# Output weights split by contraction rows, and one buffer for the normed rows, in a decoder layer on one core

## The reference, cut to what matters

```python
mix = _hybrid_mixer(h, positions, w_in[l], w_out[l])
h_res = (h_res + gate1 * _rms_norm(mix, g_post_mix[l])).astype(x.dtype)
h2 = _rms_norm(h_res, g_pre_ffn[l]) * (1.0 + scale2) + shift2
ffn = _hier_moe(h2, w_group[l], b_group[l], w_expert[l], b_expert[l],
                w_gate_exp[l], w_up_exp[l], w_down_exp[l])
h_res = (h_res + gate2 * _rms_norm(ffn, g_post_ffn[l])).astype(x.dtype)

# in _hybrid_mixer
mixed = jnp.concatenate([att.astype(h.dtype), ret], axis=-1)
return jnp.einsum('bse,ed->bsd', mixed, w_out)
```

## Time and profile before

| | |
|---|---|
| runs, median of 3 | 684.8 us (684.11 to 686.64) |
| span of the profiled execution | 686.0 us |
| PE busy | 633.2 us (92%), 2400 matmul records |
| DVE busy | 375.3 us (55%) |
| ACT busy | 206.1 us (30%) |
| moved by DMA | 174.70 MB, mean 255 GB/s |

### The profile page before, as it was taken

One profiled execution on the slowest core, in us unless ns is written; L12 is line 12 of the kernel. 1 busy time (PEld: TensorE's weight loads), 2 busy tenths in 40 slices (PEclk: granted clock), 3 DMA queues, 4 the chain that ended last, 5 costly groups with the idle time before them and its releaser, 6 DMA issues.

```text
span 686.0 us, 7088 instructions
## 1 busy us (share of the span) xinstructions
PE 633.2 (92%) x2400; PEld 298.5 (44%) x2400; DVE 375.3 (55%) x721; ACT 206.1 (30%) x411; POOL 100.3 (15%) x96
## 2 busy tenths in 40 slices
PE   1599999999999999999989999989999999988883
PEld 1364444444344444546644556433434453433331
DVE  5765667999786773246863336862323333232055
ACT  1453443334254544431121322111212121221023
POOL 1004333300122221000000000112121211110101
PEclk9999999999999999999989997999999999998998
DMA  9992715240606144070396129799999999999997
GB/s 329 394 374 96 277 28 216 59 187 7 240 0 204 43 147 162 13 241 31 125 383 289 61 86 402 269 370 409 419 421 419 420 419 420 419 418 413 409 411 157
DMA packets 52757, 174.70 MB, mean 255 GB/s; under 512 B 9712, under 2 KB 9712, under 8 KB 41840
## 3 DMA queue, kind: packets, MB, share of 16 engines
q1 hardware_dynamic: 45136, 160.26, 60.3%
q0 software_dynamic: 6160, 12.10, 5.5%
q10 hardware_dynamic: 1424, 1.87, 0.8%
HBM read 168.43 MB, written 15.21 MB: 268 GB/s over the span
## 4 chain that ended last, share of the span: by engine, by line
PE 73%; DVE 11%; DMA 7%; issue 4%; SPq 2%; ACT 1%; POOLq 0%; DVEq 0%; ACTq 0%
PE psum L772 16%; PE psum L1052 15%; PE psum L1113 8%; PE psum L775 8%; PE psum L920 7%; DMA both_bufs<-pair_rows 3%; DMA ring<-in_w_ada 2%; DVE score L1536 2%; PE psum L1025 2%; DVE sm L1535 2%; DVE score L1766 2%; SPq L647 2%; DVE rows L1459 2%; PE psum L877 2%; PE psum L897 1%
## 5 line engine op out<-in xcount | busy, mean ns | idle before, releaser
L772 PE MATMUL psum<-hT,ring 128*128 128x512 f32 (+1 forms) x320 | 135.8, 579 | 0.0
L1052 PE MATMUL psum<-ring,hT 128*64 128x512 f32 (+2 forms) x320 | 92.2, 594 | 1.8 <-DMA ring<-in_w_up_exp 1.4
L772 PEld LDWEIGHTS psum<-hT,ring 128*128 128x128 f32 x320 | 60.2, 192 | 69.4 <-issue 60.1
L775 PE MATMUL psum<-ring,hT 128*128 128x512 f32 x192 | 85.2, 597 | 0.0
L1885 DVE TENSOR_SCALAR work<-work 128x256 f32<-128x256 f32 x16 | 4.6, 290 | 101.8 <-PE psum L1062 76.0
L1248 ACT ACTIVATE both_bufs<-psum 32x512 f32<-32x512 f32 (+2 forms) x68 | 38.3, 563 | 67.7 <-PE psum L772 66.7
L1459 DVE SCALAR_TENSOR_TENSOR rows<-ring,sm,rows 128x512 f32<-128x512 f32 x64 | 55.5, 866 | 1.7
L775 PEld LDWEIGHTS psum<-ring,hT 128*128 128x128 f32 x192 | 35.6, 190 | 44.6 <-issue 44.2
L1052 PEld LDWEIGHTS psum<-ring,hT 128*64 128x64 f32 (+2 forms) x320 | 31.7, 142 | 48.8 <-issue 46.3
L1347 ACT ACTIVATE work<-psum 128x256 f32<-128x256 f32 x17 | 6.5, 383 | 146.7 <-PE psum L1052 146.7
L1113 PE MATMUL psum<-ring,work 128*64 128x512 f32 (+1 forms) x160 | 40.1, 598 | 0.7 <-ACT work L1353 0.7
(11 more groups left out here) (322 smaller groups left out, 912.9 us busy)
## 6 DMA issues: line engine op xcount, KB each, us to landing
ring<-in_w_down_exp SPq DMA_DIRECT2D x20, 1024.0 KB, 18.4
ring<-in_w_in SPq DMA_DIRECT2D x8, 2048.0 KB, 9.3
ring<-in_w_ada SPq DMA_DIRECT2D x8, 2048.0 KB, 13.8
ring<-in_w_gate_exp SPq DMA_DIRECT2D x14, 1024.0 KB, 20.2
ring<-in_w_up_exp SPq DMA_DIRECT2D x14, 1024.0 KB, 23.0
ring<-in_w_ada SPq DMA_DIRECT2D x7, 1024.0 KB, 13.3
ring<-in_w_gate_exp SPq DMA_DIRECT2D x12, 512.0 KB, 15.2
ring<-in_w_up_exp SPq DMA_DIRECT2D x12, 512.0 KB, 15.4
```

Source lines behind the costliest of these rows:

```text
L772: mm = pe.matmul(o[:, at], w[:, k, b * P:(b + 1) * P], hT3[:, k, at], start=(k == 0), stop=(k == KD - 1))
L775: mm = pe.matmul(o[:, :], hT3[:, k, b * P:(b + 1) * P], w[:, k, :], start=(k == 0), stop=(k == KD - 1))
L1052: mm = pe.matmul(o[rows, :], XT[u % 2][:, k, rows], both(GU_SLOT[place])[:, k, :, :], start=(k == 0), stop=(k == KD - 1))
```

## The change

The output weights are loaded by halves of the contraction: slot 1 holds the 512 attention rows (all 1024 columns), slot 2 the 512 retention rows. `wout(b, half)` does one half of the contraction for both banks. PE's order is new: the attention halves of blocks 0, 1 and 2 run ahead, around `turn_ret`; slot 1 is free after block 3's attention half (`wout_half`) and slot 2 after the last block. The banks of the four blocks become 4, 6, 0, 4 (they were 6, 0, 6, 0), and those of `MOD 5` and of the router follow. There is one buffer of normed rows (`H2`, in `work`), so DVE waits before each block for the store of the block before; the squares go to the buffers of `MIXN`. The tail of slot 1 is therefore free earlier, and expert 1's down weights are loaded with those of experts 0 and 3.

```diff
         for b in range(NB):
-            use(("wout", b), (6, 0)[b % 2], 2)
-        use(("MOD", 5, 0), 6)
-        use(("MOD", 5, 1), 7)
+            use(("wout", b), (4, 6, 0, 4)[b], 2)
+        use(("MOD", 5, 0), 0)
+        use(("MOD", 5, 1), 1)
...
-            use(("router", b), 4 + b % 2)
+            use(("router", b), 6 + b % 2)
...
+        def out_rows(what):
+            s = AT[("out", what)] % RING
+            return ring[:, s * SLOT:s * SLOT + KD // 2 * D].rearrange("p (k n) -> p k n", k=KD // 2)
...
-        H2 = [work[:, 2 * D:3 * D], tail(1)[:, 0:D]]
+        H2 = work[:, 2 * D:3 * D]
...
-        JUNK = tail(1)[:, D:2 * D]
...
-                    sp.dma_start(chunk(n), w_out[:, :, what * 512:(what + 1) * 512]).then_inc(landed[s], 16)
+                    half = slice(what * KD // 2, (what + 1) * KD // 2)
+                    sp.dma_start(out_rows(what), w_out[:, half, :]).then_inc(landed[s], 16)
...
-            for e in (0, 3):
+            for e in (0, 1, 3):
                 load_down(sp, e, e, down_in[e])
...
             for b in range(NB - 1):
+                if b == NB - 2:
+                    sp.wait_ge(*used_up(("out", 0)))
+                    load_gate_up(sp, 1, 1, gu_in[1])
                 sp.wait_ge(res_ready, b + 1)
                 sp.dma_start(out_blocks[b], x3[:, b, :]).then_inc(x2_out, 16)
-            for e in (1, 2):
-                sp.wait_ge(*used_up(LAST_IN[e]))
-                load_gate_up(sp, e, e, gu_in[e])
+            sp.wait_ge(*used_up(("out", 1)))
+            load_gate_up(sp, 2, 2, gu_in[2])
...
-            sp.wait_ge(h2_out[1], 16 * (NB // 2))
-            sp.wait_ge(res_sq, NB)
-            load_down(sp, 1, 1, down_in[1])
...
+                    w = out_rows(half)
                     for n in range(2):
                         o = ps[plan.bank[("wout", b)] + n]
-                        w = chunk(AT[("out", n)])
-                        for k in ks:
-                            mixed = (mixA[:, k, :] if k < 4 else hT3[:, k, :])[:, b * P:(b + 1) * P]
-                            mm = pe.matmul(o[:, :], mixed, w[:, k, :], start=(k == 0), stop=(k == KD - 1))
-                    if ks[-1] == KD - 1:
+                        for k in range(KD // 2):
+                            mixed = (mixA if half == 0 else hT3[:, KD // 2:, :])[:, k, b * P:(b + 1) * P]
+                            mm = pe.matmul(o[:, :], mixed, w[:, k, n * 512:(n + 1) * 512],
+                                           start=(half == 0 and k == 0), stop=(half == 1 and k == KD // 2 - 1))
+                    if half == 1:
                         mm.then_inc(wout_done, 1)
+                    elif b == NB - 1:
+                        mm.then_inc(wout_half, 1)
...
-                wout(0, range(KD // 2))
+                wout(0, 0)
+                wout(1, 0)
                 for b in range(NB):
                     turn_ret(b)
+                wout(2, 0)
                 pe.wait_ge(*brought(("rett", NB - 1)))
...
+                wout(0, 1)
+                wout(1, 1)
+                wout(3, 0)
+                turn_x2(0)
+                wout(2, 1)
+                route(0)
+                turn_x2(1)
+                wout(3, 1)
+                route(1)
+                turn_x2(2)
+                route(2)
                 turn_x2(NB - 1)
                 route(NB - 1)
                 mod(5)
-                pe.wait_ge(mix_n, NB)
-                stream(ps[0], 2)
+                pe.wait_ge(lg_ready, NB - 1)
+                stream(ps[6], 2)
...
-                        if b >= 2:
-                            dve.wait_ge(h2_out[b % 2], 16)
+                        if b >= 1:
+                            dve.wait_ge(h2_out[(b - 1) % 2], 16 * ((b - 1) // 2 + 1))
```

More of the change, by code:

```diff
@@ L495, in used_up @@
                 return unit_done, plan.unit[("unit", what, last_block(what))] + 1
-            return wout_done, NB
+            return (wout_half, 1) if what == 0 else (wout_done, NB)
         def rotated(kind):
@@ L907, in project, with wout @@
             def project():
-                def wout(b, ks):
-                    if b == 0 and ks[0] == 0:
-                        pe.wait_ge(att_ready, NB)
-                        land(pe, AT[("out", 0)])
-                        land(pe, AT[("out", 1)])
-                    if ks[0] == 0:
+                def wout(b, half):
+                    if b == 0:
+                        if half == 0:
+                            pe.wait_ge(att_ready, NB)
+                        land(pe, AT[("out", half)])
+                    if half == 0:
                         take(pe, ("wout", b))
+                    w = out_rows(half)
                     for n in range(2):
                         o = ps[plan.bank[("wout", b)] + n]
-                        w = chunk(AT[("out", n)])
-                        for k in ks:
-                            mixed = (mixA[:, k, :] if k < 4 else hT3[:, k, :])[:, b * P:(b + 1) * P]
-                            mm = pe.matmul(o[:, :], mixed, w[:, k, :], start=(k == 0), stop=(k == KD - 1))
-                    if ks[-1] == KD - 1:
+                        for k in range(KD // 2):
[3 more added lines that the diff above has]
+                    if half == 1:
                         mm.then_inc(wout_done, 1)
+                    elif b == NB - 1:
+                        mm.then_inc(wout_half, 1)
                 def turn_x2(b):
@@ L985, in project @@
                 mm.then_inc(early_done, 1)
-                stream(ps[0], 5)
+                stream(ps[6], 5)
             def late_rows():
@@ L1313, in _ @@
                             act.wait_ge(wout_done, b + 1)
-                            a.activation(JUNK, psum[:, w:w + D], ACT.Square, accum_out=ssm[:, b:b + 1]).then_inc(squared, 1)
+                            a.activation(MIXN[b % 2], psum[:, w:w + D], ACT.Square, accum_out=ssm[:, b:b + 1]).then_inc(squared, 1)
                             act.wait_ge(squared, 2 * b + 1)
@@ L1324, in _ @@
                             act.wait_ge(res_ready, b + 1)
-                            a.activation(JUNK, x3[:, b, :], ACT.Square, accum_out=ss2[:, b:b + 1]).then_inc(squared, 1)
+                            a.activation(MIXN[(b + 1) % 2], x3[:, b, :], ACT.Square, accum_out=ss2[:, b:b + 1]).then_inc(squared, 1)
                             act.wait_ge(squared, 2 * b + 2)
@@ L1873, in _ @@
                         link(v.reciprocal(ss2[:, b:b + 1], r2[:, b:b + 1]))
[L1874 to L1876 removed]
+                        if b >= 1:
+                            dve.wait_ge(h2_out[(b - 1) % 2], 16 * ((b - 1) // 2 + 1))
+                        link(v.scalar_tensor_tensor(out=H2, in0=x3[:, b, :], scalar=ss2[:, b:b + 1],
                                                     in1=S2, op0=ALU.mult, op1=ALU.mult))
[L1878 removed]
+                        v.tensor_tensor(H2, H2, T2, ALU.add).then_inc(h2_ready, 1)
                     routing()
```

16 lines of the change are left out of this document (2 added, 14 removed).

## The result

| | median us | runs | least to most |
|---|---|---|---|
| before | 685.07 | 4 | 684.11 to 686.64 |
| after | 678.33 | 4 | 677.93 to 680.17 |

The ratio is 0.9909, with an interval of 0.989 to 0.9928. The forecast was 677.8 us, 7.0 less than before; measured were 6.7 less (685.07 less 678.33). The profiled execution of the changed kernel has a span of 676.9 us against 686.0.

A forecast was written before the change was run, and what follows sets the result against it. Expert stage bound by weight transfers and nearly as much by PE, its start set by the chain before routing. Projection terms 0.85 + 2.31 + 1.15 + 0.69 + 1.99 = 6.99, others 0, gave 677.8 us; range 673.5 to 681.3.

The forecast's parts named there:

- Start, 0.85: Projection's start: block 0 uses banks already free and starts as the retention matmuls end, 0.85 us less.
- Wait for the retention rows, 2.31, and for the copies, 0.69: Projection: attention halves of blocks 1 and 2 fill PE's waits around the retention transposes, 2.31 and 0.69 us less.
- Transposes, 1.15: Retention transposes in the projection: 2.2 us instead of 3.37, once not paced by DVE and a slow clock; 1.15 less.
- Clock drop, 1.99: Projection matmuls behind the transposes: the 1.2 GHz stretch goes with the idle time before it, 1.99 us less, bounds 0 and -1.99.
- The router stretch, 0, with up to 3.4 more as a rival: Between projection's end (T) and routing: same stretch, 1.2 GHz drop left in place, 0; without it up to 3.4 us less.
- The buffer of normed rows, 0: DVE's wait for a store before reusing the single buffer: no wait, 0; bounds 0 and +2.6 us.
- The transfers, 0: Expert 1's weight loads issued earlier, off the chain: 0 by themselves; bounds 0 and -0.5 us.
- After the routing, everything moves by the whole: Expert stage: weight stream and PE's units both move by the whole 7.0 us; the last wait of 3.44 stays.
- (a): Rival: full clock through the router stretch, 10.4 us less in all, 674.4 us; chance 0.18.
- (b): Rival: part given back before routing, by a 2.6 us buffer wait or remaining slow clock and transposes (3.1); 680.4 to 680.9; chance 0.17.
- (c): Rival: no gain, since the weights, fully streamed from 437 us on, end the kernel whatever PE does; 684.8 us; chance 0.07.
- (d): Rival: slower, as block 2's store of normed rows falls behind 3 MB of weights; up to +9.1, 693.9 us; chance 0.04.

The follow-up runs named there:

- before, again: The kernel before the change, unchanged, run once more for a second profile: 685.26 us, ratio 0.998 to before.
- start bank: The changed kernel with block banks 6, 4, 0, 6, so block 0 again waits for ACT to empty the last retention bank: 680.01 us, ratio 0.989 to before.
- None ahead: The changed kernel with the attention halves of blocks 1 and 2 put back behind the retention transposes: 684.41 us, ratio 0.9981 to before.
- one ahead: The changed kernel with block 1's attention half ahead of the retention transposes but block 2's behind them: 679.93 us, ratio 0.9907 to before.
- order alone: The changed kernel's weight halves, banks and PE order, with normed-row buffers, squares and SP's loads as before: 678.29 us, ratio 0.9898 to before.
- buffers alone: The kernel before with one normed-row buffer, squares into `MIXN` and expert 1's down weights loaded with the first; PE's order unchanged: 686.19 us, ratio 1.0.
- changed, again: The changed kernel, unaltered, run once more for a second profile: 679.35 us, ratio 0.9908 to before.
- delay of 8: The changed kernel with eight filler matmuls added ahead of block 3's attention half: 684.88 us, ratio 0.9988 to before.
- fewer bytes: The changed kernel with half of the up weights left out in 19 expert loads, same PE matmuls, results not the reference's: 668.02 us, ratio 0.973 to before.

## Why the prediction was right, and where it was not

The forecast of 7.0 us less was met by 6.7. The mechanism in the projection is right, but that the sum came out is in part luck: the clock term was 1.9 us too large against three of the four profiles of the old order, the router stretch was put at 0 and gave some 3.5, and 0.5 to 2.2 us of it were given back behind the routing, where the sum had nothing. Against *before, again*, whose retention matmuls start within 0.05 us of the changed kernel's, the marks of the two profiles are:

| mark | before, again | changed | difference |
|---|---|---|---|
| last 40 retention records start | 335.12 | 335.17 | 0.05 |
| projection ends | 406.31 | 400.61 | -5.70 |
| first gather issued | 429.05 | 419.89 | -9.16 |
| expert 4's up weights issued | 433.90 | 424.69 | -9.21 |
| third gather issued | 448.42 | 439.27 | -9.15 |
| last wait for weights begins | 613.22 | 604.40 | -8.82 |
| last wait ends | 616.69 | 608.46 | -8.23 |
| span | 684.0 | 676.9 | -7.1 |

Step by step:

- *Start, 0.85.* Right, at 1.05: the idle 0.89 is gone, the first matmul comes 4.47 instead of 5.52 us behind the retention records' start, and *start bank* brings it back.
- *Wait for the retention rows, 2.31, and for the copies, 0.69.* Right to the last digit; both stand with the same numbers in every profile of the old order. *None ahead* brings both back (3.44 and 0.69), *one ahead* the second alone.
- *Transposes, 1.15.* Right: they take 2.26 us from 353.38 to 355.64, where 2.2 was counted, against 3.37 to 3.63 before.
- *Clock drop, 1.99.* This is the term that was mis-sized. It was read from one execution. In *before, again* the same 16 records after the same wait took 7.13 us and not 8.86. The same view gives 7.03 for 16 at full clock (the working set 8.86 against the chain's 6.87, which doesn't hold the end of the last record), so the drop cost 0.1 us there and 1.83 in the first profile:

```profile
350.05 3.62 PE L868 MATMUL psum<-cst,work 128*128 128x128 f32 x16 [2.31 <-DVE work L1835]
354.36 7.13 PE L920 MATMUL psum<-ring,hT 128*128 128x512 f32 x16 [0.69 <-ACT hT L1222]
```

```profile
354.00:357.00 3.00, 2.64 (x6) 1.25 (x7) 0.00 (x0) 0.31 (x1) 0.00 (x0) 1.00 1.00 421
```

  In two further kernels with that order it was 7.13 too, and in *none ahead*, behind a wait of 3.44, 9.59. In the four profiles of the old order the waits were the same to 0.01 us, and the clock fell in each: in *before, again* it stood at 0.50 in 350 to 352, over the transposes, and was back at 1.00 in 354 to 357, while in the first profile it was at 0.50 from 352 to 358. What differs is how much of the low stretch lies over the next 16 records. With *before, again* the gain adds up: 1.05 at the start, 0.24 for the end of the first 16 that now hides under the next, 2.31, 1.36 for the transposes, 0.69 and 0.10, in sum 5.75. So the projection's gain is 5.6 to 5.8 us against three of the four profiles of the old order and 7.2 against the first, where the sum had 6.99.
- *The router stretch, 0, with up to 3.4 more as a rival.* Here the forecast's reason was wrong. "The new order has the same stretch, with slightly more idle, so I leave the drop in place" overlooked that 32 router records in a row had become 16, 8 transposes and 16. The rival (a) came in at the first gather, at 3.1 to 3.8 us against the 3.4 worked out for it, and for another reason than the one given for it: not the moment against the clock, but the order of the work. DVE is then the later, as the working had it, and the rank matmul came at T + 12.2 as worked out. Nor did the argument from the Trainium skill help as far as it should have (TensorE: Matmul & The Clock Gate, "The HAM clock gate"): its rule is that the clock follows how busy the array was, and if PE's row is taken for that, the clock would have fallen in the new order first, where the row is 2.61 of 3 us busy, and held in the old, with 3.00 of 3. The traces show the opposite, ten times and four, so the row can't be taken for it here.

```profile
402.61:405.61 3.00, 2.61 (x25) 2.44 (x23) 2.55 (x3) 1.63 (x3) 0.00 (x0) 1.00 1.02 328
```

- *The buffer of normed rows, 0.* Right: there is no wait of DVE for a store. The store that matters, issued at 399.93, landed in 3.3 us; DVE wants the buffer 6.9 us behind the issue, at 406.84, so 3.6 us of room were left. The last store, which no buffer waits for, took 5.9 us to land among the weights, and 8.7 in *order alone* with 2 MB more issued ahead of it.
- *The transfers, 0.* Right within the intervals, as *buffers alone* and *order alone* show.
- *After the routing, everything moves by the whole.* Right for the stream's opening (-9.2) and for the third unit in the first profile, wrong as a rule. The last wait, which was to stay at 3.44, is 4.06, and 3.8 to 3.9 in four further profiles of the new order: 0.3 to 0.6 given back to the stream. It is not a wait for the last expert's weights, as the working had it: the matmuls behind it read `both_bufs` and `xs`, and loads into the ring are issued for another 15 us and more. The working also left out what stands behind it: the next 32 records take 8.4 to 10.0 us instead of 6.87 in every profile with such a wait on PE's chain, in either order, so this stall is worth 5 to 7 us in all and its price varies by 1.6. In executions where the clock stays up through the fillers, up to 1.7 more goes to the slow ranking matmuls. And the spans' difference is not all the change's: from the end of the chain (669.28) to the end of the span the first profile of the changed kernel took 7.6 us and *before, again* 6.2, and over all profiles it is 6.0 to 8.2, in either order.

So about 5.7 + 3.5 - 0.5, less up to 1.7 in a part of the executions, is 7.0 to 8.7 by the profiles; the medians say 6.7, 6.6 (*changed, again* against 685.94 beside it) and 7.9 (*order alone* against 686.21). What the executions without a profile gave back can't be seen, so the difference of a microsecond or so between the two stays open.

Of the rivals, (a) happened; (b) happened in another place than named, behind the routing and not ahead of it; (c) is refuted by *delay of 8*, though *fewer bytes* shows that the stream does set the last wait and the end; (d) had no ground, since the store landed in 3.3 us.

## What to carry to other kernels

When one engine waits at the head of a stage for another's results, put work of later blocks that needs none of them there; once the wait is covered, more work ahead brings only the next, smaller wait (4.5 us in the medians for the first half ahead; 1.0 us of the projection for the second). A clock term is to be read from several executions before it enters a sum, because the same waits cost the next 16 records 0.1 us in three and 1.8 in one. And time saved ahead of a long chain should be followed to the next place where the faster engine will now stand idle: there the clock may take part of it back.

## What the runs showed of the hardware

- Thirty-two records of 36-column float32 router matmuls in a row were followed by a fall of the granted clock from 2.4 to 1.2 GHz in four of four profiles, with PE's row full; the same 32 with eight transposes of 128 columns in their middle, and 0.4 us of idle time, in none of ten. The exchange of two calls in the program decides 3.3 to 3.7 us of the stretch. Why the clock stays up with the transposes in the middle is not shown; the idle time around them is a second difference that no run takes apart from them.
- Idle time of PE and the clock: waits of 2.31 and 0.69 us around the same transposes left the next 16 records at 7.13 us in three executions and at 8.86 in one, with 7.03 at full clock; one of 3.37 us was followed by 16 records in 3.68 us instead of 2.00 in two executions, and one of 3.36 by 2.16 in one. Behind waits of 3.4 to 4.1 us in the expert stage 32 records took 8.4 to 10.0 us instead of 6.87.
- A filler that runs at 1.2 GHz can be the better one: at 7.61 us instead of 4.54 it left PE only 0.31 us idle before work on the chain, which then took 2.00 us instead of 3.68, and the third gather came 1.7 us earlier.
